# Opening of a two-layer decoder trunk: the order of the first products, the squares and the bias row

## The chip, the core and the metric

The kernel runs on one core of one Trainium2 chip. The core has five engines that each work through their own instruction queue: TensorE (PE in the rows) multiplies, VectorE (DVE) and ScalarE (ACT) do elementwise work, GpSimd (POOL) and SyncE (SP) mostly start transfers here. Engines wait for one another only through semaphores. The metric is the device time of one execution in microseconds (us); lower is better. A difference is spoken of in per cent of the time before.

## What is computed

Two layers of a decoder trunk are run over T = 592 token columns (64 sample tokens, 16 meta tokens, 512 prompt tokens) of width 1024. Each layer begins and ends with a gated feed-forward block, and between them come four mixers. The change touches only what happens before the very first feed-forward product, and one table of attention biases that is made there:

```
def trunk_layer(h, ...):
    h = h + 0.5 * swiglu(rmsnorm(h, w['norm_ffn1']), w['ffn1_gate'], w['ffn1_up'], w['ffn1_down'])
    ...mixers...
    h = h + 0.5 * swiglu(rmsnorm(h, w['norm_ffn2']), w['ffn2_gate'], w['ffn2_up'], w['ffn2_down'])

def rmsnorm(x, g):            # y = x * rsqrt(mean(x*x) + EPS) * g
bias = rel_bias[t5_bucket(rel)]      # added to the attention scores of both layers
```

## The kernel before

**Layout.** The activations `hT` lie as 8 tiles of 128 channels by 592 columns. A half of the columns is 296. The inverse root of the norm is applied after the product, so that a product can start before the squares are summed; the gain of the norm (in `prm`, the scale factors) is applied to the operand.

**Products.** Full fp32 precision is reached by three passes: every operand is split into a high part (made by ScalarE, `x_hi`, `w_hi`) and a low part (what is left, made by VectorE, `x_lo`, `w_lo`), and TensorE multiplies high by high, low by high and high by low. In the feed-forward blocks the up and gate products of a tile are combined from seven half-size products instead of eight (a Strassen-like scheme): the operands of weights are called A11, S1, S2, S4, S3, A12 and A22, those of activations B11, T1, T2, B22, T3, B21 and T4. S and T are sums or differences that VectorE makes first (`w_sum`, `diff_rooms`, `kept_rooms`). Each product is 12 matmuls of 296 columns. The first pair of tiles runs its products in the order A11, S1, A12, S4, S2, S3, next pair's A11, A22. After it, all other pairs of the block follow in a loop, with operands made one pair ahead.

**Opening.** Nothing but loads comes ahead of it. SyncE issues the four double tiles of `hT` (semaphores `h_loaded[0..3]`) with the first four weight tiles between and behind them (`weights_loaded[0..3]`). GpSimd issues seven small loads: the scale factors `prm`, the bias table `rb` with its one-hot matrix `bucket`, then `ident`, `pages`, `ones`, `coef`. ScalarE makes high parts, and between them squares seven of the eight tiles (`first_square`, into `square_rooms`). VectorE makes differences, weight sums and low parts. TensorE first waits until all six small loads counted by `consts_loaded` have landed, makes the bias row (`rb` times `bucket`, PSUM banks 4 to 6), sums the seven squares by an identity matrix (`sum_tile(1, ident, ...)`, 14 matmuls in plain fp32, two passes each in the trace), waits until ScalarE has copied the bias row (`brow`) out of PSUM, and only then starts A11. ScalarE copies the sum of squares to `ssum`, and VectorE adds the eighth. GpSimd stores `brow` to memory and spreads it into a skewed table that attention reads much later. VectorE waits for the store of `brow` before its T3 low parts, since the feed-forward block overwrites that room.

All orders are written out by hand in the program; each engine does its instructions in exactly that order.

Of the kernel before, what the change touches and what calls it, by code (L numbers as in the profile page):

```python
# [23 lines left out]
ALU = mybir.AluOpType  # L24
# [115 lines left out]

CONSTS = 6
REL = PAST + NT
# [56 lines left out]
def build(nc, h_in, wstream, wlow, params, vbias, cache_k, cache_v, page_table, st_ret, st_gla,  # L199
# [9 lines left out]
    with ExitStack() as ctx:  # L209
        def sem(name):  # L210
            return ctx.enter_context(nc.semaphore(name))
# [220 lines left out]
        bias_row_made = sem("bias_row_made")  # L432
        bias_row_stored = sem("bias_row_stored")
        params_loaded = sem("params_loaded")
# [136 lines left out]
        def _(sp):  # L571
# [29 lines left out]
            def load_first(s):  # L601
                sp.dma_start(w_raw[:, s, :, :], wstream[s].rearrange("p (k m) -> p k m", k=8)).then_inc(weights_loaded[s], 16)

            for s in range(RING):
                sp.dma_start(hT[:, 2 * s:2 * s + 2, :], h_in[:, 2 * s:2 * s + 2, :]).then_inc(h_loaded[s], 16)
                if s < 2:
                    load_first(s)
# [81 lines left out]
        def _(pl):  # L689
            all_columns()  # L690

            def page_numbers(p):

                return [pl.value_load(pages[0:1, n:n + 1], min_val=0, max_val=POOL - 1) for n in range(2 * p * PAGES, 2 * (p + 1) * PAGES)]

            def load_values(l, numbers):

                for n, page in enumerate(numbers):
                    b2, pg = divmod(n, PAGES)
                    pl.dma_start(vpage[:, b2, pg, :], cache_v[ds(l * POOL + page, 1)].rearrange("a p n -> (a p) n")).then_inc(values_loaded[b2], 16)  # L700

            pl.dma_start(prm[:, :], params[0][:, 0:NP_ - P]).then_inc(params_loaded, 16)
            pl.dma_start(rb[0:33, :], rel_bias).then_inc(consts_loaded, 16)
            pl.dma_start(bucket[0:33, :], c_bucket).then_inc(consts_loaded, 16)
            pl.dma_start(ident[:, :], c_ident).then_inc(consts_loaded, 16)
            pl.dma_start(pages[:, :], page_table).then_inc(consts_loaded, 16)
            pl.dma_start(ones[:, :, :], c_ones).then_inc(consts_loaded, 16)
            pl.dma_start(coef[:, 0:2], c_coef).then_inc(consts_loaded, 16)
            pl.wait_ge(bias_row_made, 2)
            pl.dma_start(scratch, brow[:, :]).then_inc(bias_row_stored, 16)  # L710
            pl.wait_ge(bias_row_stored, 16)
            pl.dma_start(bass.AP(tensor=skewed.tensor, offset=skewed.offset, ap=[[H * SKEW + 1, P], [SKEW, H], [1, SKEW]]),
                         bass.AP(tensor=scratch.tensor, offset=scratch.offset + RL - SKEW, ap=[[0, P], [2 * RL, H], [1, SKEW]])
                         ).then_inc(bias_row_stored, 16)
            pl.wait_ge(bias_row_stored, 32)
            pl.sem_inc(mixers_open, 1)
            for l in range(DEPTH):
# [93 lines left out]
            pl.wait_ge(params_loaded, 16 * DEPTH)  # L811


        @block.scalar
        def _(act):
# [529 lines left out]

            def first_square(m):
                act.activation(square_rooms[:, m, :], hT[:, m, :], ACT.Square).then_inc(squared, 1)

            act.wait_ge(params_loaded, 16)
            for k in range(KH):  # L1350
                if k % 2 == 0:
                    act.wait_ge(h_loaded[k // 2], 16)
# [7 lines left out]
            for m in range(3):  # L1360
                first_square(m)
            high(0, W_S1, 0, 0, w_sum_first)
            for k in range(KH):
# [9 lines left out]
                if k == 1:  # L1373
                    first_square(4)
                    first_square(5)
                act.wait_ge(x_parts, opened("t2", k) + (LATE_PARTS if k == KH - 1 else 0))
                x_high_of("T2", k, difference_rooms(0, k)[0], 1.0)
                if k == 0:
                    first_square(3)
                    high(0, W_S2, 0, 0, w_sum_first)  # L1380
                    high(0, W_S4, 0, 0, w_sum_first)
                if k == 1:
                    act.wait_ge(h_loaded[3], 16)
                    first_square(6)
                if k == 2:
                    act.wait_ge(bias_row_made, 1)
                    act.activation(brow[:, :], ps[0:16, 4:7, :].rearrange("p b c -> p (b c)")[:, 0:RL], ACT.Copy, scale=1.0 / ATT_SCALE
                                   ).then_inc(bias_row_made, 1)
            act.wait_ge(squares_taken, 1)
            act.wait_ge(sum_cleared, 1)  # L1390
            act.activation(split_cols(ssum), pair(1), ACT.Copy).then_inc(squares_summed, SQUARED_FIRST)
            for l in range(DEPTH):
                chain[0] = 0
                ffn(l, 0, U_FFN1)
                residual(l, 0, U_DOWN1, 3, P_GAIN + 8)
                project(l)
                attention_sample(l)
                attention_prompt(l)
                retention(l)
                gla(l)  # L1400
                head_norms(l)
                branches(l)
                gates(l)
                residual(l, 8, U_OUT, 1, P_GAIN + 16)
                ffn(l, 1, U_FFN2)
                if l + 1 < DEPTH:
                    act.wait_ge(params_loaded, 16 * (l + 2))
# [7 lines left out]
        def _(pe):  # L1415
# [38 lines left out]
            def norm(l, i):  # L1454
                w = l * 3 + i
                pe.wait_ge(squares_summed, 8 * (w + 1))
                sum_tile(3, ones[:, 0, :], ssum).then_inc(square_total, 1)

            def ffn(l, f, first):
# [24 lines left out]
                def pair_(N, j, kind):  # L1484
# [30 lines left out]
                    def fifth():  # L1515
# [4 lines left out]
                        product(W_A12, BANK_B, True)  # L1520

                    if first_:
                        fifth()
# [530 lines left out]

            pe.wait_ge(consts_loaded, 16 * CONSTS)
            for n, c in enumerate(range(0, RL, 512)):
                mm = pe.matmul(ps[0:16, 4 + n, 0:min(512, RL - c)], rb[0:33, :], bucket[0:33, c:min(c + 512, RL)], start=True, stop=True)
            mm.then_inc(bias_row_made, 1)
            for n in range(SQUARED_FIRST):
                pe.wait_ge(squared, n + 1)  # L2060
                mm = sum_tile(1, ident[:, :], square_rooms[:, n, :], start=n == 0, stop=n == SQUARED_FIRST - 1)
            mm.then_inc(squares_taken, 1)
            pe.wait_ge(bias_row_made, 2)
            for l in range(DEPTH):
# [16 lines left out]
        def _(v):  # L2081
# [876 lines left out]
            for k0 in (0, 2):  # L2958
                v.wait_ge(h_loaded[k0 // 2], 16)
# [3 lines left out]
                v.wait_ge(params_loaded, 16)  # L2963
                for k in (k0, k0 + 1):
# [3 lines left out]
                if k0 == 0:  # L2968
                    v.wait_ge(h_loaded[1], 16)
                    for k in (2, 3):  # L2970
                        v.tensor_tensor(kept_rooms[:, k, 0, :], hT[:, k, span():2 * span()], hT[:, k, 0:span()], ALU.subtract).then_inc(x_parts, 1)
                    weights_here(0, 0)
                    sum_one(0, w_sum_first)
                    low(0, W_A11, 0, w_sum_first)
            sum_three(0, 0)
            for k in range(KH):
# [23 lines left out]
            v.wait_ge(bias_row_stored, 16)  # L3000
            for l in range(DEPTH):
# [206 lines left out]
```

## Time and profile before

| what | value |
|---|---|
| time, median of 3 runs | 2786.96 us (2786.23 to 2790.07) |
| profiled execution: its own time | 2791.8 us |
| profiled execution: its span | 2790.1 us |
| TensorE busy | 2767.4 us, 99% of the span |
| VectorE busy | 1985.8 us, 71% |
| ScalarE busy | 1199.4 us, 43% |
| GpSimd busy | 128.5 us, 5% |
| mean granted TensorE clock | 0.997 |

The span is the time from the first to the last instruction; the execution's own time holds 1.7 us more around it. The profiled execution is one more run beside the three: its time lies 4.8 us above their median. Shares of busy time are means over the whole span; the change lies in its first 40 us.

### The profile page before, as it was taken

What the parts mean: (1) busy time and instruction counts of PE and PEld (TensorE: products, weight loads), DVE (VectorE), ACT (ScalarE), POOL (GpSimd) and SP (SyncE); (2) the same over time, 40 slices, a digit from 0 to 9 for tenths busy, and PEclk for the clock granted to TensorE, in tenths of its full rate; (3) what the DMA queues carried; (4) which work ended last, traced back from release to release, by engine and by line L of the source; (5) the groups of instructions that cost most, each with busy time, mean ns of one, the idle gap of its engine ahead of it and who ended that gap; (6) DMA issues with size and microseconds to landing.
All of it is one profiled execution on the core that took longest, in us unless ns stands there. A gap on an engine that the chain in (4) does not pass through costs nothing.

```text
span 2790.1 us, 57892 instructions
## 1 busy us (share of the span) xinstructions
PE 2767.4 (99%) x21892; PEld 2686.3 (96%) x21892; DVE 1985.8 (71%) x3589; ACT 1199.4 (43%) x2148; POOL 128.5 (5%) x234
## 2 busy tenths in 40 slices
PE   8999999999999999999999999999999999999999
PEld 7999999998899999999999999999888999999999
DVE  8889534478667688887488895344787676899952
ACT  6445323435435254445254453234354343554521
POOL 0000001230000000000000000012300000000000
PEclk9999999999999999999999999999999999999999
DMA  4222325473334312223212223255733343122233
GB/s 139 91 94 97 110 75 198 158 204 125 104 110 173 140 65 91 90 90 114 91 66 93 90 98 106 68 198 164 220 115 117 107 178 130 61 92 104 98 106 103
DMA packets 104832, 326.01 MB, mean 117 GB/s; under 512 B 15055, under 2 KB 31855, under 8 KB 103120
## 3 DMA queue, kind: packets, MB, share of 16 engines
q1 hardware_dynamic: 91728, 280.67, 29.8%
q0 software_dynamic: 12928, 42.92, 4.8%
q8 instruction: 119, 1.95, 0.3%
q14 instruction: 57, 0.47, 0.1%
HBM read 291.51 MB, written 30.94 MB: 116 GB/s over the span
## 4 chain that ended last, share of the span: by engine, by line
PE 97%; DVE 1%; ACT 0%; DMA 0%; issue 0%; SPq 0%; DVEq 0%; ACTq 0%
PE ps L1426 52%; PE ps L1468 35%; PE ps L1652 3%; PE ps L1438 1%; PE ps L1721 1%; PE ps L1935 1%; PE ps L1771 1%; PE ps L1752 1%; PE ps L1799 0%; PE ps L1819 0%; DMA w_raw<-wstream 0%; PE ps L1703 0%; PE ps L1761 0%; PE ps L1875 0%; PE ps L1958 0%
## 5 line engine op out<-in xcount | busy, mean ns | idle before, releaser
L2087 DVE TENSOR_TENSOR w_lo<-w_raw,w_hi 128x1024 fp32r<-128x1024 f32 x240 | 292.5, 1223 | 349.6 <-ACT w_hi L822 346.1
L1468 PE MATMUL ps<-x_more,w_hi 128*128 128x296 f32 (+1 forms) x2112 | 456.8, 298 | 1.5 <-DVE x_more L2956 1.1
L1468 PE MATMUL ps<-x_hi,w_hi 128*128 128x296 f32 (+1 forms) x1408 | 419.4, 298 | 1.2 <-DVE w_lo L2125 1.2
L1468 PE MATMUL ps<-x_hi,w_lo 128*128 128x296 f32 (+1 forms) x1408 | 419.9, 298 | 0.0
L1468 PE MATMUL ps<-x_lo,w_hi 128*128 128x296 f32 (+1 forms) x1408 | 419.8, 298 | 0.0
L822 ACT ACTIVATE w_hi<-w_raw 128x1024 fp32r<-128x1024 f32 x224 | 234.9, 1053 | 407.2 <-PE ps L1426 240.5
L1426 PE MATMUL ps<-x_hi,w_hi 128*128 128x296 f32 (+1 forms) x1600 | 363.0, 308 | 3.8 <-ACT hT L1168 3.8
L2125 DVE TENSOR_TENSOR w_lo<-w_raw,w_hi 128x512 fp32r<-128x512 f32 x440 | 296.3, 688 | 88.4 <-ACT w_hi L870 85.9
L1468 PEld LDWEIGHTS ps<-x_more,w_hi 128*128 128x128 f32 x2112 | 350.6, 188 | 2.7 <-issue 1.6
L1426 PE MATMUL ps<-x_hi,w_lo 128*128 128x296 f32 (+1 forms) x1600 | 347.7, 299 | 0.0
L1426 PE MATMUL ps<-x_lo,w_hi 128*128 128x296 f32 (+1 forms) x1600 | 347.4, 298 | 0.0
L1468 PE MATMUL ps<-x_more,w_lo 128*128 128x296 f32 (+1 forms) x1056 | 314.2, 298 | 0.0
L1426 PE MATMUL ps<-hid_hi,w_hi 128*128 128x296 f32 (+1 forms) x1408 | 309.1, 298 | 0.0
L1426 PE MATMUL ps<-hid_hi,w_lo 128*128 128x296 f32 (+1 forms) x1408 | 307.6, 297 | 0.0
L1426 PE MATMUL ps<-hid_lo,w_hi 128*128 128x296 f32 (+1 forms) x1408 | 307.5, 297 | 0.0
L1426 PEld LDWEIGHTS ps<-x_hi,w_hi 128*128 128x128 f32 x1600 | 258.0, 190 | 21.3 <-issue 17.2
L920 ACT ACTIVATE p_copy<-ps 128x296 f32<-128x296 f32 (+1 forms) x264 | 109.6, 416 | 389.1 <-PE ps L1468 388.7
L870 ACT ACTIVATE w_hi<-w_raw 128x512 fp32r<-128x512 f32 x440 | 265.4, 623 | 14.1 <-PE ps L1426 13.4
L1468 PEld LDWEIGHTS ps<-x_hi,w_hi 128*128 128x128 f32 x1408 | 265.4, 189 | 2.4 <-DVE w_lo L2125 1.7
L1468 PEld LDWEIGHTS ps<-x_hi,w_lo 128*128 128x128 f32 x1408 | 265.6, 189 | 0.0
L1468 PEld LDWEIGHTS ps<-x_lo,w_hi 128*128 128x128 f32 x1408 | 264.8, 188 | 0.0
L1426 PEld LDWEIGHTS ps<-x_hi,w_lo 128*128 128x128 f32 x1600 | 260.5, 190 | 0.0
(380 smaller groups left out, 4909.5 us busy)
## 6 DMA issues: line engine op xcount, KB each, us to landing
w_raw<-wstream SPq DMA_DIRECT2D x420, 512.0 KB, 3.7
kpage<-cache_k SPq DMA_DIRECT2D x128, 128.0 KB, 3.2
vpage<-cache_v POOLq DMA_DIRECT2D x128, 128.0 KB, 3.8
gate_rows<-hT SPq DMA_DIRECT2D x48, 296.0 KB, 3.2
d_sg<-gate_rows SPq DMA_DIRECT2D x16, 888.0 KB, 4.8
h_rows<-hT SPq DMA_DIRECT2D x2, 2368.0 KB, 9.8
hT<-h_rows SPq DMA_DIRECT2D x2, 2368.0 KB, 8.7
hT<-h_in SPq DMA_DIRECT2D x4, 592.0 KB, 8.6
```

The source lines that it names most:

```text
L822: act.activation(w_hi[:, slot, :, :], w_raw[:, slot, :, :], ACT.Copy).then_inc(weights_high, 1)
L870: act.activation(w_half(t)[0], w_source(t, g, total), ACT.Copy).then_inc(operands_high, 1)
L920: act.activation(room[:, 0:span()], ps[:, bank, 0:span()], ACT.Copy).then_inc(pair_taken, 1)
L1426: mm = pe.matmul(ps[:, 2 * p + half, 0:cols], wp[:, k, :], xp[:, k0 + k - blocks[0], half * cols:(half + 1) * cols], start=start and k == ...
L1438: mm = pe.matmul(ps[:, 2 * p + half, 0:span()], mat, tile[:, half * span():(half + 1) * span()], start=start, stop=stop)
L1468: mm = pe.matmul(ps[:, bank, 0:span()], wp[:, k, :], xp, start=new and k == 0 and n == 0, stop=k == KH - 1 and n == 2, skip_group_check=True)
L1652: mm = pe.matmul(ps[0:n, (WINDOWS * g + w) % 8, 0:256], xp[:, k, c0:c0 + n], wp[:, s0:s0 + 2, k, :], start=k == 0 and m == 0, stop=k == KD ...
L1721: mm = pe.matmul(ps[0:n, score_bank(j, g, i), 0:min(ns, 512)], q, k[:, 0:min(ns, 512)], start=True, stop=True)
L1752: mm = pe.matmul(ps[r0:r0 + 32, part, :], q, kpage[:, b2, 4 * part:4 * part + 4, P * j:P * j + P], start=True, stop=True)
L1771: pe.matmul(ps[r0:r0 + 32, 5, 0:P], s_turn[:, s, r0:r0 + 32], vpage[:, b2, s, P * j:P * j + P], start=s == 0, stop=False)
L2087: v.tensor_tensor(w_lo[:, slot, :, :], w_raw[:, slot, :, :], w_hi[:, slot, :, :].bitcast(F32), ALU.subtract).then_inc(weights_low, 1)
L2125: v.tensor_tensor(lo, w_source(t, g, total), hi.bitcast(F32), ALU.subtract).then_inc(weight_steps, 1)
```

## The change

- The load of `prm` moves from GpSimd's queue to the head of SyncE's, ahead of the first activations, and counts on `h_loaded[0]`, whose first wait becomes 32.
- `rb` and `bucket` count on their own semaphore (`bias_row_moved`, also used for the store). TensorE's bias row waits for those two alone and goes to banks 5 to 7.
- TensorE does A11 and S1 before the squares (`opening_squares`, called inside `ffn`); A12 and the rest come behind them.
- The seven squares are made by GpSimd (`tensor_tensor`, `hT` times `hT`), two of them ahead of the loads of `ident`, `pages`, `ones` and `coef`, five behind.
- ScalarE gets one copy of a single element at its very start, which carries the table load, and copies the bias row right behind the high part of S1, instead of late in the opening.
- VectorE makes all eight low parts of B11 and T1 before it touches the first weights; before, four of them came behind `sum_one` and the low part of A11.

```
-            act.wait_ge(params_loaded, 16)
+            act.wait_ge(sum_cleared, 1)
+            act.activation(brow[0:1, 0:1], ssum[0:1, 0:1], ACT.Copy).then_inc(bias_row_made, 1)
...
+            sp.dma_start(prm[:, :], params[0][:, 0:NP_ - P]).then_inc(h_loaded[0], 16)
             for s in range(RING):
                 sp.dma_start(hT[:, 2 * s:2 * s + 2, :], h_in[:, 2 * s:2 * s + 2, :]).then_inc(h_loaded[s], 16)
...
+            def first_square(m):
+
+                if m % 2 == 0:
+                    pl.wait_ge(h_loaded[m // 2], 16 if m else 32)
+                pl.tensor_tensor(square_rooms[:, m, :], hT[:, m, :], hT[:, m, :], ALU.mult).then_inc(squared, 1)
...
-            pl.dma_start(prm[:, :], params[0][:, 0:NP_ - P]).then_inc(params_loaded, 16)
-            pl.dma_start(rb[0:33, :], rel_bias).then_inc(consts_loaded, 16)
-            pl.dma_start(bucket[0:33, :], c_bucket).then_inc(consts_loaded, 16)
+            pl.dma_start(rb[0:33, :], rel_bias).then_inc(bias_row_moved, 16)
+            pl.dma_start(bucket[0:33, :], c_bucket).then_inc(bias_row_moved, 16)
+            first_square(0)
+            first_square(1)
             pl.dma_start(ident[:, :], c_ident).then_inc(consts_loaded, 16)
             pl.dma_start(pages[:, :], page_table).then_inc(consts_loaded, 16)
             pl.dma_start(ones[:, :, :], c_ones).then_inc(consts_loaded, 16)
             pl.dma_start(coef[:, 0:2], c_coef).then_inc(consts_loaded, 16)
-            pl.wait_ge(bias_row_made, 2)
-            pl.dma_start(scratch, brow[:, :]).then_inc(bias_row_stored, 16)
-            pl.wait_ge(bias_row_stored, 16)
+            for m in range(2, SQUARED_FIRST):
+                first_square(m)
+            pl.wait_ge(bias_row_made, 3)
+            pl.dma_start(scratch, brow[:, :]).then_inc(bias_row_moved, 16)
+            pl.wait_ge(bias_row_moved, 48)
...
+            def opening_squares():
+
+                pe.wait_ge(consts_loaded, 16 * CONSTS)
+                for n in range(SQUARED_FIRST):
+                    pe.wait_ge(squared, n + 1)
+                    mm = sum_tile(1, ident[:, :], square_rooms[:, n, :], start=n == 0, stop=n == SQUARED_FIRST - 1)
+                mm.then_inc(squares_taken, 1)
+                pe.wait_ge(bias_row_made, 3)
...
+                    if first_ and l == 0 and f == 0:
+                        opening_squares()
                     if first_:
                         fifth()
                         fourth()
```

**VectorE, around its first weights.** These are its instructions after the second pair of differences (`kept_rooms`), before the change. `x_lo` is a low part of B11 (from `hT`) or T1 (from `kept_rooms`), `gu` the first weight sum, `w_lo` the low part of A11:

```order
L2962 TENSOR_TENSOR kept_rooms<-hT 128x296
L2956 SCALAR_TENSOR_TENSOR x_lo<-hT,prm,x_hi 128x296 [waits x_scaled,params_loaded]
...
L2971 TENSOR_TENSOR kept_rooms<-hT 128x296 [waits h_loaded_1]
L2971 TENSOR_TENSOR kept_rooms<-hT 128x296
L2130 TENSOR_TENSOR gu<-w_raw 128x512 [waits weights_loaded_1,weights_loaded_0]
L2125 TENSOR_TENSOR w_lo<-w_raw,w_hi 128x512 [waits operands_high]
L2956 SCALAR_TENSOR_TENSOR x_lo<-hT,prm,x_hi 128x296 [waits x_scaled,params_loaded,h_loaded_1]
L2956 SCALAR_TENSOR_TENSOR x_lo<-kept_rooms,prm,x_hi 128x296 [waits x_scaled,x_parts]
L2956 SCALAR_TENSOR_TENSOR x_lo<-hT,prm,x_hi 128x296 [waits x_scaled]
L2956 SCALAR_TENSOR_TENSOR x_lo<-kept_rooms,prm,x_hi 128x296 [waits x_scaled,x_parts]
L2136 TENSOR_TENSOR w_raw<-w_raw 128x512 [waits weight_steps]
```

The same place of VectorE with the change:

```order
L2973 TENSOR_TENSOR kept_rooms<-hT 128x296 [waits h_loaded_1]
L2973 TENSOR_TENSOR kept_rooms<-hT 128x296
L2959 SCALAR_TENSOR_TENSOR x_lo<-hT,prm,x_hi 128x296 [waits x_scaled,h_loaded_1]
L2959 SCALAR_TENSOR_TENSOR x_lo<-kept_rooms,prm,x_hi 128x296 [waits x_scaled,x_parts]
L2959 SCALAR_TENSOR_TENSOR x_lo<-hT,prm,x_hi 128x296 [waits x_scaled]
L2959 SCALAR_TENSOR_TENSOR x_lo<-kept_rooms,prm,x_hi 128x296 [waits x_scaled,x_parts]
L2133 TENSOR_TENSOR gu<-w_raw 128x512 [waits weights_loaded_1,weights_loaded_0]
L2128 TENSOR_TENSOR w_lo<-w_raw,w_hi 128x512 [waits operands_high]
L2139 TENSOR_TENSOR w_raw<-w_raw 128x512 [waits weight_steps]
```

Four low parts have moved from behind the first two weight instructions to ahead of them; the number of instructions is the same.

**ScalarE, the middle of its opening.** Before the change, from the high part of S1 (`w_hi<-gu`) on to the high parts of B21 (`x_more<-hT`):

```order
L1347 ACTIVATE square_rooms<-hT 128x592 x3
L870 ACTIVATE w_hi<-gu 128x512 [waits weight_steps,weights_loaded_1]
L879 ACTIVATE x_hi<-hT,prm 128x296 [waits h_loaded_2]
L879 ACTIVATE x_hi<-diff_rooms 128x296 [waits x_parts]
L1347 ACTIVATE square_rooms<-hT 128x592
...
L1347 ACTIVATE square_rooms<-hT 128x592 x2
L879 ACTIVATE x_hi<-diff_rooms 128x296 [waits x_parts]
L1347 ACTIVATE square_rooms<-hT 128x592 [waits h_loaded_3]
L879 ACTIVATE x_hi<-hT,prm 128x296 [waits h_loaded_3]
L879 ACTIVATE x_hi<-diff_rooms 128x296 [waits x_parts]
L1387 ACTIVATE brow<-ps 16x1159 [waits bias_row_made]
L879 ACTIVATE x_more<-hT,prm 128x296 x3
```

The same stretch of ScalarE with the change:

```order
L880 ACTIVATE w_hi<-gu 128x512 [waits weight_steps,weights_loaded_1]
L1370 ACTIVATE brow<-ps 16x1159 [waits bias_row_made]
L889 ACTIVATE x_hi<-hT,prm 128x296 [waits h_loaded_2]
L889 ACTIVATE x_hi<-diff_rooms 128x296 [waits x_parts]
L880 ACTIVATE w_hi<-w_raw 128x512 [waits weight_steps,weights_loaded_0]
```

The seven squares have left this queue, and the copy of the bias row has moved ahead of all operands of the second activation tiles.

**TensorE, its start.** Before the change, the bias row, the squares (14 rows in all, every second one waits for `squared`), and the first row of A11:

```order
L2057 MATMUL ps<-bucket,rb 16x512 [waits consts_loaded]
L2057 MATMUL ps<-bucket,rb 16x512
L2057 MATMUL ps<-bucket,rb 16x135
L1438 MATMUL ps<-square_rooms,ident 128x296 [waits squared]
L1438 MATMUL ps<-square_rooms,ident 128x296
...
L1468 MATMUL ps<-x_hi,w_hi 128x296 [waits weight_steps,residual_added,pair_steps,x_parts,bias_row_made]
```

TensorE's start with the change, where the dots stand for the other rows of A11, of S1 and of the squares, and the last row is the first of A12:

```order
L2065 MATMUL ps<-bucket,rb 16x512 [waits bias_row_moved]
L2065 MATMUL ps<-bucket,rb 16x512
L2065 MATMUL ps<-bucket,rb 16x135
L1474 MATMUL ps<-x_hi,w_hi 128x296 [waits weight_steps,pair_steps,residual_added,x_parts]
...
L1474 MATMUL ps<-x_hi,w_hi 128x296 [waits x_parts,residual_added,pair_steps,weight_steps]
...
L1435 MATMUL ps<-square_rooms,ident 128x296 [waits squared,consts_loaded]
L1435 MATMUL ps<-square_rooms,ident 128x296
...
L1474 MATMUL ps<-x_more,w_hi 128x296 [waits pair_steps,x_parts,weight_steps,bias_row_made]
```

The 14 matmuls of the squares now stand between S1 and A12, and A11 no longer waits for the copy of the bias row; A12 does.

## Rows read from the trace of the kernel before

**Rows 1.** The chain that ended last, whole span: shares by engine

```profile
PE 97%; DVE 1%; ACT 0%; DMA 0%; issue 0%; SPq 0%; DVEq 0%; ACTq 0%
```

**Rows 2.** The same chain to 90 us: start, length (us), what

```profile
11.34 0.12 DVE gu L2130
...
38.14 51.88 PE ps L1468 x379
```

**Rows 3.** TensorE's waits to 40 us: line, what released it, total, times, longest

```profile
PE ps L1468 <- DVE w_lo L2125: 0.9, 2, 0.6
```

**Rows 4.** Timeline of TensorE: start, length, instruction, idle time before it

```profile
11.80 4.04 PE L2057 MATMUL ps<-bucket,rb 33*16 33x512 f32 x6 [11.80 <-DMA coef<-c_coef]
15.78 8.76 PE L1438 MATMUL ps<-square_rooms,ident 128*128 128x296 f32 x28
...
27.78 0.30 PE L1468 MATMUL ps<-x_lo,w_hi 128*128 128x296 f32 x1
29.21 0.38 PE L1468 MATMUL ps<-x_more,w_hi 128*128 128x296 f32 x1 [1.13 <-DVE x_more L2956]
```

**Rows 5.** Timeline of TensorE's weight loads: the passes of the squares

```profile
17.91 0.34 PEld L1438 LDWEIGHTS ps<-square_rooms,ident 128*128 128x128 f32 x1 [0.16 <-issue]
18.41 5.66 PEld L1438 LDWEIGHTS ps<-square_rooms,ident 128*128 128x128 f32 x22 [0.16 <-issue]
```

**Rows 6.** Timeline of VectorE, around its waits in the opening

```profile
9.38 0.84 DVE L2971 TENSOR_TENSOR kept_rooms<-hT 128x296 f32<-128x296 f32 x2
11.34 0.69 DVE L2130 TENSOR_TENSOR gu<-w_raw 128x512 f32<-128x512 f32 x1 [1.12 <-DMA w_raw<-wstream]
...
12.55 0.52 DVE L2956 SCALAR_TENSOR_TENSOR x_lo<-hT,prm,x_hi 128x296 fp32r<-128x296 f32 x1
...
14.30 0.68 DVE L2136 TENSOR_TENSOR w_raw<-w_raw 128x512 f32<-128x512 f32 x1
...
24.94 1.46 DVE L2956 SCALAR_TENSOR_TENSOR x_more<-hT,prm,x_more 128x296 fp32r<-128x296 f32 x3 [0.91 <-ACT x_more L879]
...
28.54 0.52 DVE L2956 SCALAR_TENSOR_TENSOR x_more<-hT,prm,x_more 128x296 fp32r<-128x296 f32 x1
...
30.71 1.60 DVE L2171 TENSOR_TENSOR x_more<-diff_rooms,x_more 128x296 fp32r<-128x296 f32 x4 [0.84 <-ACT x_more L879]
```

**Rows 7.** Timeline of ScalarE in the opening

```profile
5.17 1.28 ACT L879 ACT_TABLE_LOAD   x1 [5.17 <-DMA hT<-h_in]
6.96 0.54 ACT L879 ACTIVATE x_hi<-hT,prm 128x296 fp32r<-128x296 f32 x1 [0.51 <-DMA prm<-params]
...
9.22 0.52 ACT L879 ACTIVATE x_hi<-hT,prm 128x296 fp32r<-128x296 f32 x1
...
10.75 0.53 ACT L879 ACTIVATE x_hi<-kept_rooms,prm 128x296 fp32r<-128x296 f32 x1
...
23.37 1.11 ACT L1387 ACTIVATE brow<-ps 16x1159 f32<-16x1159 f32 x1
```

**Rows 8.** Timelines of SyncE and GpSimd: issues of loads

```profile
0.89 0.39 SPq L605 DMA_DIRECT2D hT<-h_in  x1
2.66 0.52 POOL L704 DMA_DIRECT2D bucket<-c_bucket  x1
```

**Rows 9.** DMA issues to 20 us: KB each, us from issue to landing

```profile
ones<-c_ones POOLq DMA_DIRECT2D x1, 256.0 KB, 6.9
bucket<-c_bucket POOLq DMA_DIRECT2D x1, 149.4 KB, 6.2
```

**Rows 10.** Elementwise groups of 592 columns: instruction, operands, count, busy us, mean ns

```profile
L1347 ACT ACTIVATE square_rooms<-hT 128x592 f32<-128x592 f32 x7 | 4.5, 681 | 0.0
L2179 DVE TENSOR_TENSOR ssum<-ssum,tmp 128x592 f32<-128x592 f32 x17 | 13.1, 771 | 0.8
L2668 DVE TENSOR_TENSOR_SCAN Z<-Z 128x592 f32<-128x592 f32 x2 | 2.8, 1392 | 0.1
```

More of the change, by code:

```diff
@@ L139 @@
 NP_ = P_AW + P
-CONSTS = 6
+CONSTS = 4
 REL = PAST + NT
@@ L432, in build @@
         bias_row_made = sem("bias_row_made")
-        bias_row_stored = sem("bias_row_stored")
+        bias_row_moved = sem("bias_row_moved")
         params_loaded = sem("params_loaded")
@@ L708, in _ @@
             pl.dma_start(coef[:, 0:2], c_coef).then_inc(consts_loaded, 16)
-            pl.wait_ge(bias_row_made, 2)
-            pl.dma_start(scratch, brow[:, :]).then_inc(bias_row_stored, 16)
-            pl.wait_ge(bias_row_stored, 16)
+            for m in range(2, SQUARED_FIRST):
[3 more added lines that the diff above has]
+            pl.wait_ge(bias_row_moved, 48)
             pl.dma_start(bass.AP(tensor=skewed.tensor, offset=skewed.offset, ap=[[H * SKEW + 1, P], [SKEW, H], [1, SKEW]]),
                          bass.AP(tensor=scratch.tensor, offset=scratch.offset + RL - SKEW, ap=[[0, P], [2 * RL, H], [1, SKEW]])
-                         ).then_inc(bias_row_stored, 16)
-            pl.wait_ge(bias_row_stored, 32)
+                         ).then_inc(bias_row_moved, 16)
+            pl.wait_ge(bias_row_moved, 64)
             pl.sem_inc(mixers_open, 1)
@@ L810, in _ @@
                     pl.dma_start(prm[:, :], params[ds(l + 1, 1), :, 0:NP_ - P].rearrange("a p n -> (a p) n")).then_inc(params_loaded, 16)
-            pl.wait_ge(params_loaded, 16 * DEPTH)
+            pl.wait_ge(params_loaded, 16 * (DEPTH - 1))
         @block.scalar
@@ L1344, in opened @@
                 return OPENING_PARTS.index((name, k)) + 1
-            def first_square(m):
-                act.activation(square_rooms[:, m, :], hT[:, m, :], ACT.Square).then_inc(squared, 1)
-            act.wait_ge(params_loaded, 16)
+            act.wait_ge(sum_cleared, 1)
+            act.activation(brow[0:1, 0:1], ssum[0:1, 0:1], ACT.Copy).then_inc(bias_row_made, 1)
             for k in range(KH):
                 if k % 2 == 0:
-                    act.wait_ge(h_loaded[k // 2], 16)
+                    act.wait_ge(h_loaded[k // 2], 16 if k else 32)
                 x_high_of("B11", k, hT[:, k, 0:span()], gain_of(P_GAIN, k))
@@ L1359, in _ @@
                 side_tile(k, P_GAIN, difference_rooms(0, k)[1])
-            for m in range(3):
-                first_square(m)
             high(0, W_S1, 0, 0, w_sum_first)
+            act.wait_ge(bias_row_made, 2)
+            act.activation(brow[:, :], ps[0:16, 5:8, :].rearrange("p b c -> p (b c)")[:, 0:RL], ACT.Copy, scale=1.0 / ATT_SCALE
+                           ).then_inc(bias_row_made, 1)
             for k in range(KH):
@@ L1378, in _ @@
                 if k == 0:
-                    first_square(3)
                     high(0, W_S2, 0, 0, w_sum_first)
                     high(0, W_S4, 0, 0, w_sum_first)
[L1382 to L1388, printed above, removed]
             act.wait_ge(squares_taken, 1)
-            act.wait_ge(sum_cleared, 1)
             act.activation(split_cols(ssum), pair(1), ACT.Copy).then_inc(squares_summed, SQUARED_FIRST)
@@ L1406, in _ @@
                 if l + 1 < DEPTH:
-                    act.wait_ge(params_loaded, 16 * (l + 2))
+                    act.wait_ge(params_loaded, 16 * (l + 1))
                     act.sem_inc(phases_entered, 1)
@@ L2053, in _ @@
             pe.sem_inc(units_multiplied, RING)
-            pe.wait_ge(consts_loaded, 16 * CONSTS)
+            pe.wait_ge(bias_row_moved, 32)
             for n, c in enumerate(range(0, RL, 512)):
-                mm = pe.matmul(ps[0:16, 4 + n, 0:min(512, RL - c)], rb[0:33, :], bucket[0:33, c:min(c + 512, RL)], start=True, stop=True)
+                mm = pe.matmul(ps[0:16, 5 + n, 0:min(512, RL - c)], rb[0:33, :], bucket[0:33, c:min(c + 512, RL)], start=True, stop=True)
             mm.then_inc(bias_row_made, 1)
[L2059 to L2063, printed above, removed]
             for l in range(DEPTH):
@@ L2958, in _ @@
             for k0 in (0, 2):
-                v.wait_ge(h_loaded[k0 // 2], 16)
+                v.wait_ge(h_loaded[k0 // 2], 16 if k0 else 32)
                 if k0 == 0:
@@ L2962, in _ @@
                         v.tensor_tensor(kept_rooms[:, k, 0, :], hT[:, k, span():2 * span()], hT[:, k, 0:span()], ALU.subtract).then_inc(x_parts, 1)
-                v.wait_ge(params_loaded, 16)
                 for k in (k0, k0 + 1):
@@ L2971, in _ @@
                         v.tensor_tensor(kept_rooms[:, k, 0, :], hT[:, k, span():2 * span()], hT[:, k, 0:span()], ALU.subtract).then_inc(x_parts, 1)
-                    weights_here(0, 0)
-                    sum_one(0, w_sum_first)
-                    low(0, W_A11, 0, w_sum_first)
+            weights_here(0, 0)
+            sum_one(0, w_sum_first)
+            low(0, W_A11, 0, w_sum_first)
             sum_three(0, 0)
@@ L2999, in _ @@
                     low(0, W_S4, 0, w_sum_first)
-            v.wait_ge(bias_row_stored, 16)
+            v.wait_ge(bias_row_moved, 48)
             for l in range(DEPTH):
```

3 lines of the change are left out of this document (removed).

## The prediction

> **What bounds the kernel now.** I read the page's chain of waits first. It runs through TensorE for 97% of the span [rows 1]: work outside the opening is a matter of matmuls, and the change has the same matmuls. The same chain followed through the first 90 us [rows 2] shows where the change can act. From 38.14 us on it is one unbroken stretch of TensorE. Ahead of that, the chain is carried by VectorE and ScalarE, from the first weight sum (`gu`, 11.34 us) on. So the question is by how much the point 38.14 us moves; nothing behind it is expected to give or take, since all operands are made by the same engines in the same order there.
>
> TensorE's waits and its timeline say that this engine isn't late by its own work. It starts at 11.80 us when the last small load has landed [rows 4]. It makes the bias row and the squares to 24.5 us, runs A11 and S1 to about 28.1 us, and then stands 1.13 us for VectorE's low part of the last B21 tile, which starts at 28.54 and takes 0.52 us [rows 4, 6]. Whatever comes ahead of A12 on TensorE is therefore free as long as it ends by 29.2 us. Two more waits for VectorE's `w_lo` (0.9 us together) follow [rows 3].
>
> VectorE's timeline [rows 6] has three idle pieces from 11 us on: 1.12 us for the second weight tile, 0.91 us for ScalarE's B21 high parts, 0.84 us for ScalarE's T3 high parts. Between them it is busy. ScalarE's timeline [rows 7] explains the second: the seven squares (681 ns each, 4.5 us in all [rows 10]) and the 1.11 us copy of the bias row at 23.37 us stand in its queue ahead of B21.
>
> **Part by part.**
>
> *Scale factors first.* ScalarE loads its table at 5.17 us and starts at 6.96 us, the last 0.51 us of that for `prm` [rows 7]. With the table loaded early and `prm` at the head of SyncE's queue it starts when the first activations land. That is 5.17 plus one more issue on SyncE (0.39 us [rows 8]): about 5.6 us, 1.4 us earlier. It is worth nothing by itself. The third tile is scaled at 9.22 us [rows 7] and its activations can't have come more than a little sooner, because the same bytes are in front of it. The cover of this zero is the wait for the load; with an early load the gain could be 1.4 us at most.
>
> *Low parts ahead of the weights.* VectorE's four low parts between 12.55 and 14.30 us [rows 6] move ahead of the weight sum: 1.75 us off the chain. In their new place they follow ScalarE, which makes its last T1 part of these at 10.75 to 11.28 us [rows 7]; VectorE ends 0.5 us later, at 11.75 us. The weight sum started at 11.34 us, so it is 0.4 us later. The second weight tile is behind one more issue (0.4 us), so it lands by 11.34 + 0.4 = 11.74 us, or sooner, as `ones` (256 KB) no longer competes with it [rows 9]: in time. Net: 1.35 us gained.
>
> *Squares off ScalarE, bias copy earlier.* The 0.91 us wait for B21 goes: ScalarE has at least 4.1 us less to do before it. The 1.11 us copy now stands behind the high part of S1, at about 13.2 us. Queued behind it are the high parts of B22 and T2, for which VectorE comes at about 16.4 us, so it may be 1.6 us late before it costs. The bias product it waits for needs `bucket`, which landed at 2.66 + 6.2 = 8.9 us [rows 8, 9] and is issued no later now, plus 4.04 us on TensorE [rows 4]: done by 13.0 us. Zero. The third wait (0.84 us) stays: ScalarE's order there, `ssum` copy, two PSUM copies, then T3, is unchanged.
>
> Sum so far: 1.35 + 0.91 = 2.3 us earlier.
>
> *A11 and S1 ahead of the squares.* By itself nothing: A12 waits for VectorE, not for these two. What it buys is cover for late squares. TensorE's passes of the squares came 0.50 us apart at 18 us, then 22 in 5.66 us, 0.257 us apart [rows 5]. At the second pace the 28 passes are 7.2 us. A11 can start at 11.75 + two weight instructions = 13.0 us, S1 behind its own low part at 15.2 us; if both run at half pace, S1 ends at 18.5 us and the squares at 25.7 us. A12's operand comes at 29.06 - 2.3 = 26.8 us. So the squares fit with 1 us to spare, if GpSimd has them.
>
> *The squares on GpSimd.* This is the unknown. No row shows GpSimd computing on a tile, alone or beside VectorE. For the duration of one square I take as lower bound VectorE's own TENSOR_TENSOR of 592 columns, 771 ns, and as upper bound the dearest row of that width, the scan's 1392 ns [rows 10]. What matters for the time is what these squares take from VectorE, which reads two tiles in nearly every instruction of the opening. Lower bound zero, if the two don't meet. Upper bound the whole of all seven, if only one of the two can read at a time. I take the middle course: each square costs VectorE what it would cost on VectorE itself, 0.77 us, that being the nearest row. Seven make 5.4 us. The first two start at 5.6 us, when VectorE is ahead: without them it would be done with its first four low parts at 8.0 us (1.4 us earlier than 9.4 [rows 6]) and wait about 1.2 us for the third tile. So 4.2 us are left.
>
> Net: 4.2 - 2.3 = 1.9 us slower. The profiled execution's span is 2790.1 us and its time 2791.8 us, so it would become 2792.0 and 2793.7 us. That execution lies 4.8 us above the median of the runs; the same step on the median, 2786.96 us, gives 2788.9 us.
>
> The Trainium skill speaks against this part: in "SBUF — State Buffer", section "Who interferes with whom", a VectorE instruction with two SBUF inputs and a GpSimd instruction that reads SBUF exclude each other, and the later one blocks for the whole of the other. "GPSIMD Engine Reference", section 3.1, gives 4497 ns for a 2048-element fp32 tensor_tensor; by that a square is an estimated 1.3 us, and the sum would be 7 x 1.3 - 1.2 - 2.3 = 5.6 us slower. No row here bears on either.
>
> **The rivals.**
>
> *No interference.* GpSimd and VectorE pass each other by. Then only the gain is left: 2784.7 us. For it: they are separate engines with separate queues, and nothing in the program orders a square against VectorE's work. Against it: GpSimd never worked on a tile in this trace, so there is no row that shows it. It also needs the last square in time. GpSimd has two squares, four issues at 0.52 us [rows 8], then five squares from about 5.6 us on: 7.7 us plus seven squares, one more us on TensorE, against 26.8 us. Up to 2.5 us each they are hidden. 0.29.
>
> *Whole exclusion with slow squares* (the other side). While a square runs, VectorE stands, at 1.39 us each: 9.7 - 1.2 = 8.5 us lost, 2.3 gained, so 6.2 us slower, 2793.2 us. For it: VectorE's opening is busy but for its waits [rows 6], so every collision lands on the chain. Against it: nothing in this trace, but nothing shows it either. It decides from 0.5 us per square, where the gain is used up. This is what the skill's rule above would do. 0.25.
>
> *Starved squares.* VectorE, whose instructions follow one another without a gap, keeps GpSimd out, and five squares run only when VectorE first pauses, near 27.5 us. Five times 1.39 is 34.5 us, one more on TensorE 35.5 us, and A12 starts 6.3 us later than at 29.21 us, with ScalarE's `ssum` copy and so T3 behind it: 2793.3 us. The store of the bias row waits behind the squares on GpSimd too, and VectorE waits for the store before T3. 0.08.
>
> *A large gain.* Over 5.6 us would need more than all of VectorE's waits after 11 us (2.87 us) and the 1.75 us together. 0.04, for what the measurement may add.
>
> *The forecast.* 0.34.
>
> **How the numbers follow.** About 0.2%, 5.6 us, is what a measurement of this kernel can tell from no change. The forecast and the rival without interference lie within it, 0.63, and I add 0.05 for exclusion with squares somewhat shorter than the upper bound: 0.68 same. Slower by more: 0.28. Faster by more: 0.04. The range reaches from just under the case without interference to just over the two slow cases, 2783.5 to 2794.0 us.
>
> **What the changed profile would show.** Right: a first weight sum at 11.7 us and no 0.91 us wait on VectorE before B21; ScalarE at 5.6 us; A11 near 13 us if no squares are in the way; TENSOR_TENSOR rows on GpSimd, and beside them VectorE rows longer than 0.52 or 0.68 us by about 0.8 us per square; the unbroken stretch of TensorE from about 40 us. Unchanged VectorE durations and a start at 35.8 us mean no interference. A start past 43 us means exclusion. I would be wrong in another way if TensorE idled before a row of the squares, or if ScalarE's copy of the bias row came after 15 us.

## The result, and the profile after

The changed kernel takes 2793.71 us (median of 22 runs, 2788.8 to 2798.83), the kernel before 2790.05 us (22 runs, 2784.03 to 2791.78) on the same chips. The ratio is 1.0017, its 95% interval 1.0011 to 1.0023: some 4.7 us slower, between 3.1 and 6.4 (the means lie 4.7 us apart, the medians 3.7). The profiled execution has a span of 2791.2 us and a mean granted clock of 0.999, against 2790.1 us and 0.997 before.

Those two spans differ by 1.1 us only, and the chain of waits says how that goes with 4.7. The chain of the changed kernel to 90 us (start, length, what):

```profile
10.72 5.05 DVE x_lo L2959
15.77 1.73 DVE kept_rooms L2973 x2
...
19.25 0.60 DVE gu L2133
...
43.63 46.44 PE ps L1474 x339
```

TensorE's unbroken stretch starts at 43.63 us; it started at 38.14 [rows 2]. The opening has lost 5.49 us. Behind that point the changed execution took 2747.6 us, the one before 2752.0 us, though that part of the kernel is the same. Over the ten profiled executions of this document this rest goes with the mean granted clock of the execution: 2744.6 to 2744.9 us at 1.000, 2747.6 to 2747.8 at 0.999, 2752.0 and 2752.1 at 0.997. I call the start of the stretch S from here on and judge every kernel by it first.

VectorE's timeline of the changed kernel has the place of the loss:

```profile
5.83 1.82 DVE L2965 TENSOR_TENSOR kept_rooms<-hT 128x296 f32<-128x296 f32 x2 [3.92 <-DMA hT<-h_in]
7.57 1.43 DVE L2959 SCALAR_TENSOR_TENSOR x_lo<-hT,prm,x_hi 128x296 fp32r<-128x296 f32 x1
8.93 0.51 DVE L2959 SCALAR_TENSOR_TENSOR x_lo<-kept_rooms,prm,x_hi 128x296 fp32r<-128x296 f32 x1
9.36 1.43 DVE L2959 SCALAR_TENSOR_TENSOR x_lo<-hT,prm,x_hi 128x296 fp32r<-128x296 f32 x1
10.72 5.05 DVE L2959 SCALAR_TENSOR_TENSOR x_lo<-kept_rooms,prm,x_hi 128x296 fp32r<-128x296 f32 x1
15.69 1.81 DVE L2973 TENSOR_TENSOR kept_rooms<-hT 128x296 f32<-128x296 f32 x2
...
19.17 0.68 DVE L2133 TENSOR_TENSOR gu<-w_raw 128x512 f32<-128x512 f32 x1
...
36.22 1.60 DVE L2174 TENSOR_TENSOR x_more<-diff_rooms,x_more 128x296 fp32r<-128x296 f32 x4 [1.28 <-ACT x_more L889]
```

An instruction of 296 columns takes 0.52 us [rows 6]. Here two take 1.43 us, one takes 5.05 us, and the differences, 0.84 us a pair before, take 1.82 us. None of this is shown as a wait: the engine counts as busy. Nor is there a semaphore between the two engines here, so the sentence ahead of the prediction that engines wait for one another only through semaphores does not hold: GpSimd holds VectorE up without one. The first weight sum starts at 19.17 us instead of 11.34. GpSimd's timeline of the changed kernel lies beside it:

```profile
5.88 2.80 POOL L701 TENSOR_TENSOR square_rooms<-hT 128x592 f32<-128x592 f32 x2 [3.24 <-DMA hT<-h_in]
...
10.86 5.93 POOL L701 TENSOR_TENSOR square_rooms<-hT 128x592 f32<-128x592 f32 x5
```

Five squares run in 5.93 us, and within them VectorE ends one instruction. All in all VectorE's rows up to 17.5 us are longer by 8.30 us. ScalarE, which reads what VectorE makes, stands too, and on TensorE the first product is what is late. ScalarE's timeline, then TensorE's, of the changed kernel:

```profile
5.83 0.54 ACT L889 ACTIVATE x_hi<-hT,prm 128x296 fp32r<-128x296 f32 x1 [3.45 <-DMA hT<-h_in]
...
17.16 0.54 ACT L889 ACTIVATE x_hi<-kept_rooms,prm 128x296 fp32r<-128x296 f32 x1 [7.58 <-DVE kept_rooms L2973]
```

```profile
8.14 4.04 PE L2065 MATMUL ps<-bucket,rb 33*16 33x512 f32 x6 [8.14 <-DMA bucket<-c_bucket]
20.71 0.59 PE L1474 MATMUL ps<-x_hi,w_hi 128*128 128x296 f32 x1 [8.53 <-DVE w_lo L2128]
...
26.50 7.14 PE L1435 MATMUL ps<-square_rooms,ident 128*128 128x296 f32 x28
34.27 0.37 PE L1474 MATMUL ps<-x_more,w_hi 128*128 128x296 f32 x1 [0.63 <-DVE x_more L2959]
```

The 28 passes of the squares still end before A12 can start (0.63 us idle), so their new place on TensorE costs nothing.

The sum closes: the weight sum is 7.83 us later; the four low parts of 1.75 us no longer come behind it; the 0.91 us wait before B21 is gone; the wait before T3 is 1.28 us instead of 0.84 [rows 6], 0.44 more. 7.83 - 1.75 - 0.91 + 0.44 = 5.61, against 5.49 measured.

### The profile page after: what moved, and what is told of

Read it like the earlier page. It is cut to its first block, busy times and chain, and to the rows that moved or that the text cites. A ratio compares the mean times of both kernels' runs of the same rounds, so it can differ in the third digit from the quotient of the medians.

```text
span 2791.2 us, 57895 instructions
## 1 busy us (share of the span) xinstructions
PE 2763.6 (99%) x21892; PEld 2683.9 (96%) x21892; DVE 1994.4 (71%) x3589; ACT 1195.8 (43%) x2142; POOL 136.6 (5%) x240
## 3 DMA queue, kind: packets, MB, share of 16 engines
q8 instruction: 119, 1.95, 0.3%
## 4 chain that ended last, share of the span: by engine, by line
PE 97%; DVE 2%; ACT 0%; issue 0%; DMA 0%; SPq 0%; DVEq 0%; ACTq 0%
PE ps L1423 51%; PE ps L1474 35%; PE ps L1660 3%; PE ps L1435 1%; PE ps L1729 1%; PE ps L1943 1%; PE ps L1779 1%; PE ps L1760 1%; PE ps L1807 0%; PE ps L1827 0%; DVE x_lo L2959 0%; PE ps L1711 0%; PE ps L1769 0%; PE ps L1883 0%; PE ps L1966 0%
## 6 DMA issues: line engine op xcount, KB each, us to landing
hT<-h_rows SPq DMA_DIRECT2D x2, 2368.0 KB, 11.2
```

## The experiments

Theory: a GpSimd square and a VectorE instruction that reads two tiles shut each other out for the whole of the square (some 1.2 us); without that the change is 1 to 2 us faster. Rival one: the squares cost little, and the order of VectorE or the early bias copy is what loses. Rival two: GpSimd's being busy at all does it, whatever it does.

**Squares back on ScalarE**, all else as changed: the function of the squares and its calls go back to where they stood.

```
-                pl.tensor_tensor(square_rooms[:, m, :], hT[:, m, :], hT[:, m, :], ALU.mult).then_inc(squared, 1)
+                act.activation(square_rooms[:, m, :], hT[:, m, :], ACT.Square).then_inc(squared, 1)
```

> The changed kernel with the seven squares back on ScalarE at their old places; all else as changed. I read the start of TensorE's unbroken stretch (38.1 us before, 43.6 us changed). Theory 1, all of the loss is VectorE standing while GpSimd squares: VectorE's rows are back to 0.46 to 0.68 us, the first weight sum starts near 11.7 us, the stretch near 35.8 to 36.5 us, and the time is about 2 us (0.1%) under the kernel before. Theory 2, part of the loss comes from the new order (first two products at half pace, copy of the bias row in ScalarE's way): the stretch starts at 38 us or later.

Measured: 2787.77 us beside 2788.67, ratio 0.999 (0.9981 to 0.9999); S is 37.13 us, between the two theories and outside the range of either. VectorE's rows are back at 0.52 and 0.68 us. Its timeline in this kernel shows a wait that wasn't there before:

```profile
11.87 0.68 DVE L2135 TENSOR_TENSOR gu<-w_raw 128x512 f32<-128x512 f32 x1
...
15.31 0.69 DVE L2130 TENSOR_TENSOR w_lo<-gu,w_hi 128x512 fp32r<-128x512 f32 x1 [0.55 <-ACT w_hi L870]
```

Three squares stand ahead of ScalarE's high part of S1, and now that VectorE comes for it earlier, it waits. The change without its squares on GpSimd is slightly faster than before, so the loss comes from them alone, and rival one has fallen.

**Only the squares moved**, in the kernel before:

```
-                act.activation(square_rooms[:, m, :], hT[:, m, :], ACT.Square).then_inc(squared, 1)
+                pl.tensor_tensor(square_rooms[:, m, :], hT[:, m, :], hT[:, m, :], ALU.mult).then_inc(squared, 1)
```

> The kernel before with nothing changed but the seven squares, made by GpSimd: two behind the loads of the bias row, five behind the other loads. Theory 1: GpSimd's 8.7 us of squares hold VectorE up, less what its waits there take in (1.66 us for the first scaled tile, 1.12 us for the weights, 0.91 us for B21): the stretch starts near 38.1 + 8.7 - 3.7 = 43.1 us, and the time is 5 us over before. Theory 2, it takes the new order too: the stretch stays within 1 us of 38.1 us.

Measured: 2793.69 us, ratio 1.0015 (1.0006 to 1.0024); S is 42.80 us, 4.66 later. VectorE's timeline in this kernel:

```profile
10.44 2.79 DVE L2969 TENSOR_TENSOR kept_rooms<-hT 128x296 f32<-128x296 f32 x2
13.14 1.66 DVE L2128 TENSOR_TENSOR gu<-w_raw 128x512 f32<-128x512 f32 x1
14.72 1.66 DVE L2123 TENSOR_TENSOR w_lo<-w_raw,w_hi 128x512 fp32r<-128x512 f32 x1
16.30 1.43 DVE L2954 SCALAR_TENSOR_TENSOR x_lo<-hT,prm,x_hi 128x296 fp32r<-128x296 f32 x1
17.65 0.52 DVE L2954 SCALAR_TENSOR_TENSOR x_lo<-kept_rooms,prm,x_hi 128x296 fp32r<-128x296 f32 x1
```

and GpSimd's:

```profile
10.10 7.30 POOL L706 TENSOR_TENSOR square_rooms<-hT 128x592 f32<-128x592 f32 x5
```

Here the two take turns: the two differences, the sum, the low part and the next low part (five instructions) are longer by 1.95, 0.98, 0.98 and 0.91 us, and the five squares take 7.30 instead of 5.93 us since they wait too. The row at 17.65, behind the last square, has its normal length. The sum at 13.14 and the low part at 14.72 us read weights, not `hT`, so it is not the tile that GpSimd reads that VectorE has to wait for. The 0.91 us wait before B21 is still there, so taking the squares off ScalarE does not remove it:

```profile
29.61 1.46 DVE L2954 SCALAR_TENSOR_TENSOR x_more<-hT,prm,x_more 128x296 fp32r<-128x296 f32 x3 [0.91 <-ACT x_more L889]
```

**Five more squares** on GpSimd, to rooms that nobody reads:

```
+                if m > 1:
+                    pl.tensor_tensor(more_rooms[:, m - 2, :], hT[:, m, :], hT[:, m, :], ALU.mult)
```

> The changed kernel with five more squares on GpSimd (each of the last five is also written to a room that nobody reads). Theory 1: every square that GpSimd makes while VectorE has work costs its whole length, 1.19 us: the stretch starts 5.9 us later, near 49.5 us, and one VectorE instruction takes some 11 us instead of 5.05. Theory 2, the two share the time and the long instruction is the price of one collision: less than 2 us later.

Measured: 2799.99 us, ratio 1.004 (1.0025 to 1.0055); S is 49.35 us, 5.72 later than with seven: 1.14 us for each square added. In VectorE's timeline of this kernel nearly all of it stands in one instruction:

```profile
10.83 10.67 DVE L2963 SCALAR_TENSOR_TENSOR x_lo<-kept_rooms,prm,x_hi 128x296 fp32r<-128x296 f32 x1
```

**A memset in place of each square.** GpSimd writes the same rooms at the same places and reads nothing; the kernel leaves the squares out.

```
-                pl.tensor_tensor(square_rooms[:, m, :], hT[:, m, :], hT[:, m, :], ALU.mult).then_inc(squared, 1)
+                pl.memset(square_rooms[:, m, :], 1.0).then_inc(squared, 1)
```

> The changed kernel with each square replaced by GpSimd's memset of the same room to one, so that GpSimd writes and reads nothing; the sum of squares in the first norm is then a constant. Theory 1a, the two collide only where both read: VectorE's rows have their usual length, the stretch starts near 35.8 us. Theory 1b, any GpSimd instruction on these tiles keeps VectorE out: VectorE rows are longer by the memsets' lengths, and the stretch starts later by their sum (if 0.5 us each, near 38 to 39 us).

Measured: 2787.22 us, ratio 0.9991 (0.9982 to 1.0); S is 36.02 us. GpSimd's timeline and, behind it, VectorE's:

```profile
5.66 1.12 POOL L701 MEMSET square_rooms<- 128x592 f32 x2 [3.03 <-DMA hT<-h_in]
9.08 1.12 POOL L701 MEMSET square_rooms<- 128x592 f32 x2 [0.18 <-DMA hT<-h_in]
```

```profile
9.05 0.84 DVE L2973 TENSOR_TENSOR kept_rooms<-hT 128x296 f32<-128x296 f32 x2 [0.83 <-DMA hT<-h_in]
9.81 0.52 DVE L2959 SCALAR_TENSOR_TENSOR x_lo<-hT,prm,x_hi 128x296 fp32r<-128x296 f32 x1
...
11.56 0.68 DVE L2133 TENSOR_TENSOR gu<-w_raw 128x512 f32<-128x512 f32 x1
```

A memset beside each of the rows at 9.05 us leaves them at their normal length. The weight sum comes 7.61 us earlier than with squares (19.17), and S comes 7.61 us earlier (43.63): that is the net toll of seven squares, to the last digit carried through to TensorE. Net, because the 0.83 us wait for the third tile takes in a part of the 8.30 us. Rival two has fallen.

**A copy in place of each square**, which reads one tile instead of two operands; the squares are left out.

```
+                pl.tensor_copy(square_rooms[:, m, :], hT[:, m, :]).then_inc(squared, 1)
```

> The changed kernel with each square replaced by GpSimd's copy of the tile, one input instead of two; the first norm then sums the activations and not their squares. Theory 1, one input that is read is enough: VectorE's rows are longer by the copies' lengths; with copies half as long as squares the stretch starts 4 us later than with memsets, near 40 us. Theory 2, it takes two inputs on both sides: VectorE's rows have their usual length, the stretch starts near 36 us.

Measured: one run, 2784.49 us, too few to judge the time by; S is 38.22 us, 2.20 later than with the memset. From GpSimd's timeline, then VectorE's:

```profile
9.63 1.67 POOL L701 COPY square_rooms<-hT 128x592 f32<-128x592 f32 x2
11.74 1.71 POOL L701 COPY square_rooms<-hT 128x592 f32<-128x592 f32 x2 [0.44 <-DMA hT<-h_in]
```

```profile
9.82 0.93 DVE L2959 SCALAR_TENSOR_TENSOR x_lo<-hT,prm,x_hi 128x296 fp32r<-128x296 f32 x1
10.68 0.93 DVE L2959 SCALAR_TENSOR_TENSOR x_lo<-kept_rooms,prm,x_hi 128x296 fp32r<-128x296 f32 x1
11.53 0.51 DVE L2959 SCALAR_TENSOR_TENSOR x_lo<-hT,prm,x_hi 128x296 fp32r<-128x296 f32 x1
11.97 0.93 DVE L2959 SCALAR_TENSOR_TENSOR x_lo<-kept_rooms,prm,x_hi 128x296 fp32r<-128x296 f32 x1
12.83 1.16 DVE L2133 TENSOR_TENSOR gu<-w_raw 128x512 f32<-128x512 f32 x1
```

A copy takes 0.84 to 0.9 us and holds VectorE for 0.42 to 0.48 us of it, about half. All seven copies do so, 3.1 us together, of which the wait for the third tile takes in a part. What GpSimd reads makes the toll; a copy's toll is only part of its length, a square's nearly the whole. Why it is a part stays open: GpSimd's spans are rough. I had expected a start near 40 us.

**Only the bias copy early**, in the kernel before (ScalarE copies the bias row behind the high part of S1):

```
+            act.wait_ge(bias_row_made, 1)
+            act.activation(brow[:, :], ps[0:16, 4:7, :].rearrange("p b c -> p (b c)")[:, 0:RL], ACT.Copy, scale=1.0 / ATT_SCALE
...
```

> The kernel before with only ScalarE's copy of the bias row moved to right behind the high part of S1. Theory 1, it was this copy that made VectorE wait 0.91 us for B21: the wait is gone and the stretch starts near 37.2 us instead of 38.1. Theory 2, the squares made the wait: it stays over 0.5 us and the stretch within 0.4 us of 38.1.

Measured: one run, 2788.46 us; S is 37.15 us, 0.99 earlier. VectorE has no wait before B21, with the squares still on ScalarE:

```profile
23.97 1.44 DVE L2955 SCALAR_TENSOR_TENSOR x_more<-hT,prm,x_more 128x296 fp32r<-128x296 f32 x3
```

So the copy alone makes that gain.

**Only VectorE's order**, in the kernel before (four low parts ahead of the weight sum, which leaves the loop over them):

```
-                    weights_here(0, 0)
-                    sum_one(0, w_sum_first)
-                    low(0, W_A11, 0, w_sum_first)
+            weights_here(0, 0)
+            sum_one(0, w_sum_first)
+            low(0, W_A11, 0, w_sum_first)
```

> The kernel before with only VectorE's order changed: all low parts of B11 and T1 ahead of the first weights. Theory 1, its worth is the 1.35 us of the prediction wherever it stands: the stretch starts at 36.8 us. Theory 2, in the kernel before ScalarE's three squares stand in front of the high part of S1 and VectorE then waits for that: 37.5 us, with a new wait of 0.7 us on VectorE before the low part of S1.

Measured: one run, 2784.01 us; S is 37.50 us, 0.64 earlier. The timeline of VectorE has the same new wait as with the squares back on ScalarE:

```profile
15.24 0.69 DVE L2125 TENSOR_TENSOR w_lo<-gu,w_hi 128x512 fp32r<-128x512 f32 x1 [0.55 <-ACT w_hi L870]
```

**The changed kernel with squares on ScalarE, placed in its waits**: the version that these runs point to. One square goes behind the copy of the bias row, none stands ahead of S1's high part, and the others go between the high parts of the second tiles.

```
+            first_square(0)
...
+                if k == 1:
+                    for m in (2, 3, 4):
+                        first_square(m)
+                if k == 2:
+                    first_square(5)
+                    first_square(6)
...
                 if k == 0:
+                    first_square(1)
```

> The changed kernel with the squares on ScalarE, but each where ScalarE waits for VectorE when it has no squares: one behind the copy of the bias row, one behind the first T2 part, three behind the second B22 part, two behind the third. Without any squares in VectorE's or ScalarE's way the stretch started at 36.0 us, with them at their old places at 37.1 us. Theory 1, the 1.1 us between is the three squares in front of the high part of S1 and what follows from them: the stretch starts at 36.0 to 36.3 us, and the time is 2 us (0.07%) under the kernel before. Theory 2, ScalarE has no room for 4.1 us of squares anywhere: 37 us or later.

Measured: 2787.69 us beside 2788.4, ratio 1.0002 (0.9992 to 1.0011); S is 36.53 us, 1.61 earlier than before, with neither the wait for S1 nor that before B21. That misses the 36.0 to 36.3 us of theory 1. The 0.51 us that it starts later than the memset kernel is there already when the third tile lands (9.05 us there):

```profile
9.56 0.84 DVE L2974 TENSOR_TENSOR kept_rooms<-hT 128x296 f32<-128x296 f32 x2 [1.30 <-DMA hT<-h_in]
```

1.6 us is 0.06%, and this ratio can't tell it from nothing. Compared at one clock, as in the last column below, the times lean to the version too.

The kernels with more than one run, ranked by S. The third column is the ratio's excess over 1, times 2790 us. The last compares executions of the same mean granted clock only: those of the kernel before that the experiments were measured beside took 2791.2 us on average at 0.997, 2789.3 at 0.998, 2786.8 at 0.999 and 2784.1 at 1.000 (10, 17, 13 and 2 executions), so most of the spread within one kernel goes with the clock.

| kernel | S moved by | time moved by | time moved by, at one clock (0.997 to 1.000) |
|---|---|---|---|
| five more squares | +11.21 | +11.2 | +11.5 to +12.4 |
| the change | +5.49 | +4.7 | +4.8 to +5.5 |
| only the squares moved | +4.66 | +4.2 | +4.2 to +5.4 |
| squares back on ScalarE | -1.01 | -2.8 | -0.8 to -0.2 |
| squares in ScalarE's waits | -1.61 | +0.6 | -1.9 to -0.8 |
| memset in place of squares | -2.12 | -2.5 | -1.8 to -1.6 |

Each shift of S lies within the interval of its ratio, and at one clock the times follow S to 1.3 us. A microsecond in the opening is about a microsecond at the end.

## Why the prediction was right or wrong

The sign was right, and so was the place: GpSimd's squares lengthen VectorE's rows, and everything else is a small gain. The size was off: 1.9 us forecast, about 4.7 in the times and 5.49 at S. That 2793.7 us lies inside the range is in part luck: the range was built on 2786.96 us, and beside the change the kernel before took 2790.05.

- *The squares on GpSimd.* This is the term that was mis-sized. I took 0.77 us for each from VectorE, the middle between none and all, "that being the nearest row", and 4.2 us in all. The runs show 8.30 us in VectorE's rows where I had 5.4, 7.61 us net where I had 4.2, 1.14 us for each further square, and rows longer by 0.91 to 0.98 us even where the two engines take turns. The nearest row told how long VectorE needs for such a square; what counts is how long GpSimd holds the other, and that is its own time. The middle had no mechanism behind it. The rival of whole exclusion named a start past 43 us as its sign, and it is 43.63. It had the mechanism; only its 1.39 us a square was somewhat dear (mean 1.287 us in the group of GpSimd's squares).
- In the same part I allowed 1.2 us that the wait for the third tile would hide. It was 0.83 us, by the memset kernel.
- The Trainium skill ("SBUF — State Buffer", section "Who interferes with whom") spoke against this part: a VectorE instruction with two SBUF inputs and a GpSimd instruction that reads SBUF exclude each other, one that only writes does not. The 5.05 us row and the memset kernel's 0.52 us rows agree with both halves. Two things lie outside it: that row spans several squares and not one, and a copy held VectorE for only half of its length. That it takes two inputs on VectorE's side no run here shows. The estimate that the prediction made with it, 5.6 us slower, lies next to the 5.49 us measured, in part because errors cancel: the 9.1 us for the seven squares were 8.30 us in VectorE's rows, and the 1.2 us hidden were 0.83. I gave the whole exclusion 0.25, as no row of the kernel before bore on it.
- *Scale factors first, worth nothing.* ScalarE did start earlier (5.83 instead of 6.96 us), on the chip slightly later than the 5.6 us I gave. In the memset kernel VectorE then waits 0.83 us for the third tile, so the head start is used up there, as said.
- *Low parts ahead of the weights, 1.35 us.* Right in the change as a whole, where ScalarE makes the high part of S1 early: the weight sum starts at 11.56 us in the memset kernel, the rest follows without a wait. Alone it is worth 0.64 us, since 0.55 us comes back as a wait for S1's high part behind three squares.
- *Squares off ScalarE, bias copy earlier, 0.91 us.* The wait is gone, but one of my two reasons was idle: moving the squares alone left it, moving the copy alone removed it. *The third wait stays* held for the kernels built on the one before (0.84 us); in the changed one and the five others built on it it is 1.27 to 1.29 us.
- *The sum without interference, 2.3 us earlier, S at 35.8 us.* The memset kernel has 36.02.
- *A11 and S1 ahead of the squares as cover.* Right: the cover held even with squares that ended at 16.8 us and TensorE at half pace. It had little to do, since VectorE's delay moved A11 as well.

What stays open: the 0.44 us before T3. In the changed kernel VectorE starts T3 at 36.22 us, 0.55 us after ScalarE's first T3 part (35.22, 0.45 us long) has ended; before it was about 0.1 us. The early bias copy alone and the VectorE order alone don't bring it, nor do GpSimd's squares. I did not try the new semaphore, the load of `prm` or TensorE's order singly. Open too is the row at 9.36 us in the changed kernel, 1.43 us long: GpSimd's records show issues of loads beside it, no square. The two other kernels with squares on GpSimd have such a row as well, 1.46 us at 9.05 (only the squares moved) and 1.43 us at 9.47 (five more squares); the memset and copy kernels have none beside the same issues. GpSimd's spans are rough; what these rows met isn't settled, and their 0.9 us is part of the net 7.61.

## What to carry to other kernels

Before work goes to an idle engine, ask what it shares with the busy one: here a square on GpSimd costs VectorE nearly its whole length and a copy about half, while a memset, which only writes, costs nothing, so the idle engine was no free room. Where no row shows what a shared resource costs, price both ends and choose by the mechanism; a middle that no mechanism gives is a guess. Sort times by the granted clock before you call a difference of 0.1% unreadable. And before moving work off an engine to end a wait, find the one instruction that is ahead in its queue: the copy, not the seven squares, was what held B21, and moving it alone brought S forward by 0.99 us without touching GpSimd.

## What was new about the hardware

- A run of GpSimd squares can starve VectorE altogether. Beside five squares back to back one VectorE instruction took 5.05 us, beside ten 10.67 us; yet in the kernel where only the squares moved the engines took turns, one for one. I found no rule in the traces for which of the two happens. In all VectorE's rows grew by 8.30 us in the first case and by 7.1 us in the second.
- VectorE's lost time is booked as busy: the page gives it 1994.4 us in the changed kernel, 8.6 more than before with the same 3589 instructions. A view of waits shows none of it; only mean durations do.
- TensorE ran at half pace where the granted clock reads full. After 8.5 us without matmuls, the passes of A11 and most of S1, up to the row at 25.78 us, start 0.247 us apart; that is 296 columns at 1.2 GHz. Later ones come 0.137 us apart, near the 0.123 us of 2.4 GHz. The windows view of the changed kernel, over the idle stretch and the slow one (granted clock in the third column from the end), and TensorE's timeline at the turn:

```profile
12.20:20.70 8.50, 0.00 (x0) 0.02 (x1) 8.50 (x10) 3.54 (x8) 4.59 (x4) 1.00 0.43 164
20.70:25.70 5.00, 4.99 (x20) 5.00 (x21) 4.93 (x10) 3.59 (x7) 1.33 (x2) 1.00 0.09 15
```

```profile
25.54 0.45 PE L1474 MATMUL ps<-x_hi,w_lo 128*128 128x296 f32 x1
25.78 0.45 PE L1474 MATMUL ps<-x_lo,w_hi 128*128 128x296 f32 x1
26.03 0.36 PE L1474 MATMUL ps<-x_hi,w_hi 128*128 128x296 f32 x1
26.22 0.30 PE L1474 MATMUL ps<-x_hi,w_lo 128*128 128x296 f32 x1
26.36 0.30 PE L1474 MATMUL ps<-x_lo,w_hi 128*128 128x296 f32 x1
```

It cost nothing here, as TensorE still waited 0.63 us before A12. The pace of the passes is the surer sign of the clock in such a short stretch.
